# Retention stage: the transposed keys and the score products made once per chunk pair and used for both scan directions

## The reference, cut to what matters

```python
    scores = jnp.einsum('bcihk,bcjhk->bchij', q, k) * dmask
    o_in = jnp.einsum('bchij,bcjhv->bcihv', scores, v)
    kv = jnp.einsum('bcjhk,jh,bcjhv->cbhkv', k, k_dec, v)
    def step(s, kv_c):
        return chunk_decay * s + kv_c, s
    s_fin, s_prev = lax.scan(step, s0, kv)
    o_x = jnp.einsum('bcihk,ih,cbhkv->bcihv', q, q_dec, s_prev)
    return (o_in + o_x).reshape(b_, n, RET_HEADS, RET_DV), s_fin
```

## Time and profile before

| | before |
|---|---|
| time of 3 runs, us | 4568.11, 4568.91, 4576.76; median 4568.91 |
| profiled execution, us | 4571.26, of which the span 4569.5 |
| PE busy | 3741.4 us (82%) |
| DVE busy | 2791.1 us (61%) |
| ACT busy, POOL busy | 1640.7 us (36%), 1622.7 us (36%) |
[...]
| transfers | 1672.73 MB, 366 GB/s |

### The profile page before, as it was taken

How to read it: one execution, slowest core, us unless ns; L and a number is a source line. 1 busy time by engine, 2 the same in 40 slices (tenths; PEclk the granted TensorE clock), 3 DMA queues, 4 the chain that set the end, 5 groups by cost and what they waited for, 6 DMA issues and landing times.

```text
span 4569.5 us, 44582 instructions
## 1 busy us (share of the span) xinstructions
PE 3741.4 (82%) x12065; PEld 1568.4 (34%) x12065; DVE 2791.1 (61%) x6341; ACT 1640.7 (36%) x5133; POOL 1622.7 (36%) x1312
## 2 busy tenths in 40 slices
PE   8999999999998689999776887888777556666666
PEld 6654455656553233443221232342222111011110
DVE  1122776577676976654898566545678984544544
ACT  4211345232213343334344333333343553333333
POOL 0000132223222333333434434443444445555554
PEclk9999999999999799999887998999877676666666
DMA  8645688789999989999999989999999999999998
GB/s 343 228 166 214 261 336 324 272 305 378 373 406 401 366 353 402 382 377 411 398 394 340 420 350 405 400 400 409 401 400 383 395 397 415 413 421 415 415 421 349
DMA packets 277883, 1672.73 MB, mean 366 GB/s; under 512 B 30528, under 2 KB 48000, under 8 KB 91136
## 3 DMA queue, kind: packets, MB, share of 16 engines
q0 software_dynamic: 184320, 1342.26, 73.3%
q1 hardware_dynamic: 85152, 304.18, 17.3%
q10 hardware_dynamic: 8160, 23.43, 1.6%
HBM read 1631.98 MB, written 37.78 MB: 365 GB/s over the span
## 4 chain that ended last, share of the span: by engine, by line
PE 44%; DMA 29%; DVE 14%; issue 7%; ACT 4%; POOL 2%; DVEq 0%; ACTq 0%; SPq 0%; POOLq 0%
DMA slots<-in_peer,idxR 27%; PE ps L1394 27%; PE ps L1412 9%; DVE slots L1701 4%; PE ps L1387 4%; POOL slots L1098 2%; ACT lhs L1153 1%; ACT wgts L1145 1%; DVE ti L1721 1%; DVE ti L1718 1%; DMA counts<-in_mlat 1%; DVE tv L1720 1%; PE ps L1518 1%; DVE rest L1719 1%; ACT gelus L1142 1%
## 5 line engine op out<-in xcount | busy, mean ns | idle before, releaser
L1098 POOL DMA_INDIRECT slots<-in_peer,idxR x1280 | 1616.4, 1263 | 2871.8 <-PE ps L1412 1779.8
L1412 PE MATMUL ps<-slots,lhs 128*64 128x512 f32 x4544 | 1483.1, 767 | 725.2 <-ACT lhs L1153 722.7
L1701 DVE CUSTOM_DVE_ANT_0 slots<-slots,h2R 128x1024 f32<-128x1024 f32 x1280 | 1546.2, 1223 | 763.8 <-issue 706.5
L1394 PE MATMUL ps<-ring,arena 128*128 128x512 f32 (+1 forms) x3264 | 1365.1, 575 | 15.2 <-ACT arena L1353 6.5
L1412 PEld LDWEIGHTS ps<-slots,lhs 128*64 128x64 f32 x4544 | 294.8, 158 | 1811.2 <-ACT lhs L1153 1582.3
L1394 PEld LDWEIGHTS ps<-ring,arena 128*128 128x128 f32 x3264 | 623.2, 195 | 769.8 <-issue 752.3
L1142 ACT ACTIVATE gelus<-dots 128x1 f32<-128x1 f32 x1280 | 256.5, 200 | 1509.6 <-DVE dots L1701 1505.5
L1153 ACT ACTIVATE lhs<-fold,wgts 128x64 f32<-128x64 f32 x1136 | 395.1, 348 | 37.2
L1145 ACT ACTIVATE wgts<-gelus,gsmR 128x1 f32<-128x1 f32 x1280 | 377.2, 295 | 42.4 <-ACT gelus L1142 0.5
L1394 PE MATMUL ps<-ring,slots 128*128 128x512 f32 (+1 forms) x576 | 221.6, 545 | 0.0
L1713 DVE SCALAR_TENSOR_TENSOR slots<-slots,wgts 128x1024 f32<-128x1024 f32 x135 | 172.9, 1281 | 79.0 <-ACT wgts L1145 73.0
(11 more groups left out here) (206 smaller groups left out, 2420.2 us busy)
## 6 DMA issues: line engine op xcount, KB each, us to landing
ring<-in_whead SPq DMA_DIRECT2D x48, 1024.0 KB, 9.6
ring<-in_wa SPq DMA_DIRECT2D x48, 1024.0 KB, 9.2
ring<-in_wq SPq DMA_DIRECT2D x32, 1024.0 KB, 16.2
slots<-in_peer,idxR POOLq DMA_INDIRECT x1280, 13.1
ring<-in_wgc SPq DMA_DIRECT2D x16, 1024.0 KB, 9.5
ring<-in_wgb SPq DMA_DIRECT2D x16, 1024.0 KB, 9.9
ring<-in_wout SPq DMA_DIRECT2D x16, 1024.0 KB, 14.8
o_scratch<-inb SPq DMA_DIRECT2D x80, 128.0 KB, 5.2
```

What stands on the lines that cost most here:

```text
L1098: g.indirect_dma_start(out=slot(R), out_offset=None, in_=a["peer"], in_offset=bass.IndirectOffsetOnAxis(ap=idxR[:, p % KEEP, g2, col:col + ...
L1394: done = mm(out, lhsT, rhs, start=n == 0, stop=n == KD - 1)
L1412: done = mm(ps[j * HALF:(j + 1) * HALF, g2, :], weights, slot(R)[:, D + j * UW:D + (j + 1) * UW], start=start, stop=stop)
L1701: v.tensor_tensor_reduce(out=u, in0=u, in1=h2R[:, g2, :], scale=1.0, scalar=0.0, op0=ALU.mult, op1=ALU.add, accum_out=dots[:, R % LHS:R % ...
```

## The change

In the first half of the iterations (`it < nch // 2`) sA still transposes k and multiplies q and k for both chunks. Its results are now used twice. ACT multiplies the transposed k with both directions' decays: two results into `kd` as before, and two, with the directions swapped, into a new tile `kd2` that keeps them for iteration n-1-it. DVE masks the scores for this iteration into `sm`, releases `sm_done`, then masks them with the other direction's mask and writes them over the two chunks of k in `kT`, which are no longer needed. In the second half sA has no PE and no ACT part; DVE makes only `qd`. sB then takes the masked scores from `kT` and the decayed k from `kd2`. The bank of the scores is now released after the second masking. The event costs that place the rows change too: of the second half of sA from 1.9 to 0.5.

```diff
             def first(it):
-                ev = self.add("sA", 2, g=G_, h=h, i=it, z=self.scans, pe=1.9, act=.6, dve=1.0)
+                if it < nch // 2:
+                    ev = self.add("sA", 2, g=G_, h=h, i=it, z=self.scans, pe=1.9, act=1.2, dve=1.5)
+                    self.at["kt", G_, h, it] = self.at["kt", G_, h, nch - 1 - it] = ev.t
+                else:
+                    self.add("sA", g=G_, h=h, i=it, z=self.scans, dve=.5)
                 self.scans += 1
...
+        kd2 = view(13 * D + UW, D, "p (i r n) -> p i r n", i=4, r=2)
...
                     for r in range(2):
-                        e = A_(kd[:, ev.i % 2, r, :], bank(t)[:, r * P:(r + 1) * P], ACT.Copy,
+                        A_(kd[:, ev.i % 2, r, :], bank(t)[:, r * P:(r + 1) * P], ACT.Copy,
+                           scale=kdec[:, r * HEADS + ev.h:r * HEADS + ev.h + 1])
+                    for r in range(2):
+                        e = A_(kd2[:, ev.i, r, :], bank(t)[:, (1 - r) * P:(2 - r) * P], ACT.Copy,
                                scale=kdec[:, r * HEADS + ev.h:r * HEADS + ev.h + 1])
                     e.then_inc(freed[t % BANKS], 1)
...
-                elif k == "sA":
+                elif k == "sA" and t >= 0:
...
+                    half = len(STAGES[ev.g]) // 2
                     for r in range(2):
                         out = bank(t)[:, r * DV:(r + 1) * DV]
-                        mm(out, sm[:, ev.i % 2, r * P:(r + 1) * P], vv[ev.g][:, cs[r], :], start=True, stop=False)
+                        masked = (sm[:, ev.i % 2, r * P:(r + 1) * P] if ev.i < half else
+                                  kT[ev.g][:, cs[r] * P:(cs[r] + 1) * P])
+                        mm(out, masked, vv[ev.g][:, cs[r], :], start=True, stop=False)
...
-                        done = mm(bank(t + 1)[:, r * DV:(r + 1) * DV], kd[:, ev.i % 2, r, :], vv[ev.g][:, cs[r], :],
+                        decayed = kd[:, ev.i % 2, r, :] if ev.i < half else kd2[:, 2 * half - 1 - ev.i, r, :]
+                        done = mm(bank(t + 1)[:, r * DV:(r + 1) * DV], decayed, vv[ev.g][:, cs[r], :],
                                   start=True, stop=True)
...
+                    if t < 0:
+                        st.settle()
+                        dve.sem_inc(s["sm_done"], 1)
+                        continue
                     filled(dve, t + 1)
                     st.link(v.tensor_tensor(sm[:, b, :], bank(t + 1)[:, 0:2 * P], decays[:, 0:2 * P], ALU.mult))
+                    dve.sem_inc(s["sm_done"], 1)
+                    for r in range(2):
+                        c = mirrored(ev.g, ev.i, 1 - r)
+                        st.step(v.tensor_tensor(kT[ev.g][:, c * P:(c + 1) * P], bank(t + 1)[:, (1 - r) * P:(2 - r) * P],
+                                                decays[:, r * P:(r + 1) * P], ALU.mult))
+                    st.settle()
                     dve.sem_inc(freed[(t + 1) % BANKS], 1)
-                    dve.sem_inc(s["sm_done"], 1)
```

More of the change, by code:

```diff
@@ L240, in first @@
             def first(it):
-                ev = self.add("sA", 2, g=G_, h=h, i=it, z=self.scans, pe=1.9, act=.6, dve=1.0)
+                if it < nch // 2:
[3 more added lines that the diff above has]
+                    self.add("sA", g=G_, h=h, i=it, z=self.scans, dve=.5)
                 self.scans += 1
-                self.at["kt", G_, h, it] = ev.t
-                self.at["sc", G_, h, it] = ev.t + 1
             for i in range(nch // 2):
```

## The result

| | before | after |
|---|---|---|
| median of 6 runs, us | 4568.51 | 4583.42 |
| lowest and highest, us | 4566.92, 4576.76 | 4580.24, 4585.90 |
| profiled execution, us | 4571.26, span 4569.5 | 4582.43, span 4580.7 |
| mean granted PE clock, share of full speed | 0.871 | 0.863 |

The ratio is 1.0032, with a 95% interval of 1.0020 to 1.0043: slower by 9 to 20 us. The prediction gave slower a chance of 0.12, and its range ended at 4577.

A forecast was written before the change was run, and what follows sets the result against it. PE was taken to bound the program up to 1250 us, with transfers at 0.99 in the last 869 us. Terms -2.9 + 1.1 - 0.9 - 4.1 + 2.1 = -4.7 us took 4568.9 to 4564.2 us, range 4554 to 4577.

The forecast's parts named there:

- The step that failed: Behind the latent retention, 970 to 1250 us: rows falling up to 3 behind were taken to cost nothing.
- level again in the query products of group 1: Rows up to 3 behind at the first `z` (113 instead of 116) would have caught up by there.
- The fourth rival: Gathers, not PE, pace 1250 us and later, so no gain arrives: 4568.9 us, chance 0.13.
- Context: Context retention, 54 to 158 us: PE spared one sA of 0.72 us in each of four heads, -2.9 us.
- Heads 0 and 1: Latent retention, rows accumulated on PE: +1.1 us in head 0 and -0.9 us in head 1.
- The state's step: Latents: sB(i+1) needs sB(i)'s state, 3.97 us without sA, so a removed sA gives 0.45 us, not 0.72.
- Heads 2 and 3: Latent retention, rows chained on DVE, which sets the step: -4.1 us in head 2, +2.1 us in head 3.
- a row paid elsewhere: Row accumulation leaving a latent head's loop or idle time costs PE about 1.0 us elsewhere.
- The large term: Head 2 of the latents: shorter stall, -1.9 us, and shorter sB(1) to sB(7), -2.1 us; -4.1 us taken.
- the full gain: Rival: DVE keeps up and no idle times come, 14.4 us gained, 4554.5 us, chance 0.16.
- the clock: Rival: PE at half clock in thinner latent steps, 2.0 us each; 4604 us if 20 fell, chance 0.07.
- DVE's pace: Rival: DVE paces all four latent heads, +4.6 us, 4573.5 us, or 4579.6 at the upper bound; chance 0.14.

The follow-up runs named there:

- old work, new places: The kernel before with only the cost of the second half of sA lowered from 1.9 to 0.5, moving the rows: 4584.59 us, ratio 1.0038.
- changed work, old places: The changed kernel with the second half of sA kept at cost 1.9, so rows stand as before: 4569.09 us against 4565.83, ratio 1.0007.

## Why the prediction was wrong

**The step that failed.** "As 970 to 1250 us moves with PE, and they cost PE nothing there, I take nothing." The rows' delay was seen, priced at 2.9 us a row "if gathers paced it", and set to zero. Its measured price is 15 us. Of these, 3.6 arise between 967 and 1060 us, where PE waits 2.5 us longer for ACT's copy into `tmp`; the rows of the kernel before and of the changed one:

```profile
PE ps L1387 <- ACT tmp L1313: 3.4, 2, 2.4
```

```profile
PE ps L1393 <- ACT tmp L1319: 5.9, 2, 4.8
```

and 9.8 between 1172 and 1513 us, a stretch of which the prediction read only the first 78 us. The share of 0.93 from 970 to 1250 us was no sign that transfers leave room there: it is a mean over two stretches, and in the last 78 us of them it was already 1.00 at 406 GB/s; from 1172 to 1513 us it is 1.01 at 404 GB/s. The assumption that rows are "level again in the query products of group 1" was true and no comfort: the time is lost on the way there. That late rows cost only what their transfers cost was the second half of the wrong step: three rows at 2.9 us would be 8.7 us. The fourth rival ("the gathers, not PE, pace 1250 us and later") named the transfers, but only as something that eats a gain, never as something that makes later rows dearer. The last sentence of the prediction, that it is wrong if the part behind 970 us changes by more than 3 us, is what happened.

**Context, -2.9 forecast, -0.2 measured.** A head's period, from the first large projection product behind one head to that behind the next, was 27.93 us before:

```profile
73.07 7.15 PE L1394 MATMUL ps<-slots,ring 128*128 128x256 f32 x32
...
101.00 1.33 PE L1394 MATMUL ps<-slots,ring 128*128 128x256 f32 x5
```

and 27.81 us after:

```profile
65.10 1.07 PE L1451 MATMUL ps<-arena,slots 128*32 128x256 f32 x16 [0.77 <-DMA arena<-in_wlate]
...
70.50 7.15 PE L1400 MATMUL ps<-slots,ring 128*128 128x256 f32 x32
...
92.92 1.07 PE L1451 MATMUL ps<-h2R,slots 128*32 128x256 f32 x16 [0.33 <-DMA h2R<-in_wlate]
...
98.31 3.92 PE L1400 MATMUL ps<-slots,ring 128*128 128x256 f32 x17
```

0.12 us of the 0.72 arrive, and over three heads (products 64 to 256) 0.17: 85.77 to 85.60 us. The bracket shows why: the modulation weights are now waited for. At the modulation products ahead of the wait PE is 0.66 us earlier in its period (21.01 instead of 21.67 us), at those behind it 0.14. That PE was busy for 100.8 of 104 us was no proof that nothing else stood just behind it.

**Heads 0 and 1.** The state's step was read rightly. In head 0 from sB(3) on, and sB(7):

```profile
620.17 0.67 PE L1527 MATMUL ps<-arena 128*128 128x256 f32 x2 [0.20 <-DVEq L1914]
...
624.21 0.67 PE L1527 MATMUL ps<-arena 128*128 128x256 f32 x2 [0.20 <-DVEq L1914]
...
628.25 0.67 PE L1527 MATMUL ps<-arena 128*128 128x256 f32 x2 [0.20 <-DVEq L1914]
...
632.29 0.67 PE L1527 MATMUL ps<-arena 128*128 128x256 f32 x2 [1.21 <-DVEq L1914]
```

4.04 us each (forecast 3.97), with 0.20 us of idle PE where a row stands in the step and 1.21 where none does (forecast 0.2 to 0.3, and 1.3). sB(1) to sB(7) took 26.27 us (forecast 26.4), its stall 4.74 us (above 4.0). In head 1 it took 27.95 us (forecast 26.8), mainly because the first step behind the stall was 7.46 us, not 6.49:

```profile
729.55 1.19 PE L1527 MATMUL ps<-arena,tmp 128*128 128x256 f32 x2 [5.65 <-DVEq L1914]
...
737.01 0.60 PE L1527 MATMUL ps<-arena,tmp 128*128 128x256 f32 x2
```

**Heads 2 and 3.** DVE's part of a first-half step of head 2:

```profile
842.15 0.87 DVE L1908 SCALAR_TENSOR_TENSOR arena<-arena,gch,ps 128x256 f32<-128x256 f32 x2
843.37 0.49 DVE L1882 TENSOR_TENSOR tmp<-arena 128x128 f32<-128x128 f32 x2 [0.35 <-issue]
843.78 0.42 DVE L1889 TENSOR_TENSOR tmp<-ps,arena 128x256 f32<-128x256 f32 x1
844.35 0.49 DVE L1893 TENSOR_TENSOR arena<-ps,arena 128x128 f32<-128x128 f32 x2
845.05 1.28 DVE L1723 SCALAR_TENSOR_TENSOR slots<-slots,wgts 128x1024 f32<-128x1024 f32 x1 [0.22 <-DVE arena L1893]
```

The second masking takes 0.49 us and 0.21 to the next operation, 0.70 against the 0.80 that was taken. A first-half step is 5.24 us (forecast 5.47), a second-half one 4.23 to 4.28 with a row and 4.04 without (forecast 4.34, 3.97). Head 2's stall fell to 1.02 us and its products ran in 0.67 us, as forecast:

```profile
838.08 0.67 PE L1527 MATMUL ps<-arena,tmp 128*128 128x256 f32 x2 [1.02 <-DVEq L1914]
...
843.32 0.67 PE L1527 MATMUL ps<-arena,tmp 128*128 128x256 f32 x2 [1.75 <-DVEq L1914]
...
848.57 1.19 PE L1527 MATMUL ps<-arena,tmp 128*128 128x256 f32 x2 [2.42 <-DVEq L1914]
...
854.16 0.67 PE L1527 MATMUL ps<-arena 128*128 128x256 f32 x2 [1.21 <-DVEq L1914]
```

From sB(1) to sB(7) head 2 took 28.64 us (forecast 27.9) and head 3 28.89 (28.3). In each, one step alone makes the difference: from sB(3) to sB(4), forecast at 4.34 us, 5.59 (848.57 to 854.16) and in head 3 5.73. Behind the long wait of the first half's last step (2.42 and 2.38 us) PE's granted clock was 0.50: in head 2 from 848.57 to 851.26 us, up to just before the kv products, which the state waits for, and in head 3 from 944.33 to 946.03 us, with 0.62 during the kv products.

The scan of a head, from its last product of values (L1394 or L1400) to the first large projection product behind it, in us, each from one trace; the forecast is without the 1.0 us that heads 0, 1 and 3 were charged for a row paid elsewhere:

| head | before | after | difference | forecast | old work, new places | changed work, old places |
|---|---|---|---|---|---|---|
| 0 | 45.07 | 43.51 | -1.6 | +0.1 | 45.38 | 45.76 |
| 1 | 45.95 | 47.56 | +1.6 | -1.9 | 45.88 | 43.46 |
| 2 | 41.19 | 37.20 | -4.0 | -4.1 | 35.65 | 41.92 |
| 3 | 36.47 | 38.22 | +1.8 | +1.1 | 36.81 | 35.91 |

Four other traces with the changed kernel's retention differ from it by up to 1.8 us in a head. The large term, head 2, came out at its number, but the rows bring it and not the spared work: DVE has 7 chained rows in that scan instead of 9, the old work with the same 7 is at least as fast, and the changed work with 9 gains nothing. In head 1 the forecast gain did not come. The scans together give back 2.2 us, the rest of the retention costs 2.5 (the rows paid elsewhere, 3.0 in the forecast), which makes +0.3 from product 704 to product 1664 where -1.8 was forecast. That the two are only 2 us apart is in part luck: the misses of heads 0 and 1, -1.7 and +3.5, go against each other. Together with the context the forecast was -4.7 us. The kernel with the rows at their old places shows no gain, its ratio 0.9998 to 1.0016, against the 0.9990 that -4.7 us would be. Of the rivals, the full gain did not come, the clock fell in two thin steps and not in 20, and DVE's pace held only in heads 2 and 3, as counted.

## What to carry to other kernels

Where a planner places independent work by costs written in the events, editing a cost is a change of its own: price the moved work over the whole length on which it is moved, until it is level again, and run it alone, with the old work. Read the transfers' share for the whole of that stretch and in parts, not just as a mean over its beginning. Do not take the price of one moved row as the row's transfer: here one row cost 9.7 us in one pattern, and three 15 us in another, in other stretches. Relief of the busiest engine is worth only what the next waiter leaves, so look at the loads that arrive just in time and at loops through another engine before multiplying spared instructions by their length.

## What was not expected of the hardware

In the thin steps the first products take 0.67 us, at a granted clock of 1.00 (616 to 635, 741 to 760, 854 to 869 and 949 to 964 us), behind idle times of 0.20 to 1.45 us, one in nearly every step, over whole heads; behind 1.02 to 1.79 us in the first halves of heads 2 and 3 the clock was 1.00 too (838 to 846 and 933 to 940 us). Behind 2.42 us in head 2 they took 1.19 us: from 848.57 to 851.26 us the clock was 0.50, and the fourth group of products, 0.83 us, still ran at 0.65. In head 3, behind 2.38 us, the first group took 0.67 us at 1.00 and the third 1.06 us at 0.50. In the rows read of the kernel before, the products of 1.19 us had stood only behind 3.58 us and more (a clock of 0.50 from 730.26 to 733.50 and from 840.79 to 843.50 us), and behind 4.00 us in head 0 the first products still took 0.67 us at 1.00, those behind them 0.90 and 1.06 at 0.61 and 0.50. The length of the wait alone does not decide it: with the changed work at the old places, products behind 2.41 us in head 2 took 1.04 us, at a clock of 0.52 from 852.78 to 856.17 us, and all behind 2.38 us in head 3 took 0.59 to 0.67, at 1.00. A fall cost 1.3 to 1.5 us (steps of 5.59 and 5.73 against 4.23 to 4.28), since the state's loop contains it, and the next step was at 1.00 again. Of the 26 waits for the state in the latents of the changed kernel, the clock fell behind the four longest only: the stalls of 4.74 and 5.65 us (0.50 from 606.02 to 608.50 and from 729.55 to 732.50 us), and the 2.42 and 2.38 us.
